# Reading the samples' matrix memories with the queries as a padded stationary operand, and asking for memory rows sooner

## The reference, cut to what matters

```python
qk = jnp.einsum('bthd,bshd->btsh', qc, kc) * W
num = jnp.einsum('btsh,bshd->bthd', qk, vc) + g[..., None] * jnp.einsum('bhvk,bthk->bthv', C, qc)
den = jnp.sum(qk, axis=2) + g * jnp.einsum('bhk,bthk->bth', n, qc)
hc = num / jnp.maximum(jnp.abs(den), jnp.exp(-mt))[..., None]
C = gl[..., None, None] * C + jnp.einsum('bsh,bshv,bshk->bhvk', wl, vc, kc)
```

## Time and profile before

| | |
|---|---|
| median of three runs | 2119.77 us (2115.84 to 2128.39) |
| profiled execution, its own time | 2122.74 us |
| its span, first to last instruction | 2120.9 us |
| PE busy | 1957.2 us, 92% of the span |
| DVE, ACT busy | 1316.9 us (62%), 937.2 us (44%) |
| mean granted clock of TensorE | 0.923 of full speed |

### The profile page before, as it was taken

One profiled execution on the slowest core, in us unless ns is written; L12 is line 12 of the kernel. 1 busy time (PEld: TensorE's weight loads), 2 busy tenths in 40 slices (PEclk: granted clock), 3 DMA queues, 4 the chain that ended last, 5 costly groups with the idle time before them and its releaser, 6 DMA issues.

```text
span 2120.9 us, 28589 instructions
## 1 busy us (share of the span) xinstructions
PE 1957.2 (92%) x10524; PEld 1564.2 (74%) x10524; DVE 1316.9 (62%) x1730; ACT 937.2 (44%) x1259; POOL 120.1 (6%) x162
## 2 busy tenths in 40 slices
PE   5999998799999998999968897999999999999994
PEld 3666665699977477777744585888888888888883
DVE  4352452488742245778833325888888888888884
ACT  0122220000001014676734412777777777777772
POOL 0000000000010000000000001110111100111001
PEclk8999966899999978999979876999999999999997
DMA  4422622445556123333369642999999999999992
GB/s 166 159 80 80 188 65 49 135 161 185 159 167 224 40 79 120 120 125 120 130 224 341 216 144 79 333 358 368 341 338 345 351 361 361 339 336 347 360 374 81
DMA packets 194853, 453.19 MB, mean 214 GB/s; under 512 B 11931, under 2 KB 77591, under 8 KB 193466
## 3 DMA queue, kind: packets, MB, share of 16 engines
q1 hardware_dynamic: 187970, 423.00, 56.6%
q0 software_dynamic: 6784, 28.88, 4.4%
HBM read 439.04 MB, written 21.27 MB: 217 GB/s over the span
## 4 chain that ended last, share of the span: by engine, by line
PE 84%; DVE 8%; DMA 3%; issue 3%; SPq 2%; ACT 1%; POOL 0%; DVEq 0%; POOLq 0%; ACTq 0%
PE bank L2357 76%; PE bank L2360 8%; SPq L2224 1%; DMA arena<-in_cache_nsa 1%; DVE arena L1525 1%; ACT arena L2920 1%; DVE arena L2722 0%; DVE uT L2657 0%; DMA arena<-in_x_sample 0%; DMA arena<-in_cache_nsa_win 0%; DMA ring<-in_cache_nsa 0%; DVE rtmp L2650 0%; DVE arena L2645 0%; DMA ring<-scr_y,mem_all 0%; ACT L2920 0%
## 5 line engine op out<-in xcount | busy, mean ns | idle before, releaser
L2357 PE MATMUL bank<-arena_r 128*128 128x448 f32 (+2 forms) x3296 | 813.1, 361 | 16.8 <-DVE uT_r L652 10.1
L2357 PEld LDWEIGHTS bank<-arena_r 128*128 128x128 f32 x3296 | 607.6, 189 | 92.9 <-issue 15.4
L1810 DVE TENSOR_TENSOR ring_r<-ring,arena_r 128x1792 fp32r<-128x1792 f32 (+1 forms) x216 | 443.6, 2088 | 47.6 <-ACT arena_r L2920 46.3
L2920 ACT ACTIVATE arena_r<-ring 128x1792 fp32r<-128x1792 f32 (+1 forms) x216 | 370.1, 1726 | 164.3 <-PE bank L2357 133.8
L2920 ACT ACTIVATE arena<-bank 64x256 f32<-64x256 f32 (+12 forms) x419 | 179.0, 437 | 446.3 <-PE bank L2357 231.8
L2357 PE MATMUL bank<-arena 128*128 128x256 f32 (+20 forms) x1626 | 275.1, 357 | 6.1 <-ACT arena L2920 3.5
L2357 PE MATMUL bank<-ring_r,arena_r 128*128 128x448 f32 (+1 forms) x840 | 246.1, 374 | 0.0
L2357 PEld LDWEIGHTS bank<-arena 128*128 128x128 f32 (+13 forms) x1626 | 195.8, 182 | 63.0 <-issue 38.0
L2357 PEld LDWEIGHTS bank<-ring_r,arena_r 128*128 128x128 f32 x840 | 157.7, 188 | 21.6
L2360 PE MATMUL bank<-consts_sb,arena 128*128 128x128 f32 (+7 forms) x792 | 134.0, 303 | 40.9 <-DMA arena<-in_x_sample 10.8
L1810 DVE TENSOR_TENSOR arena_r<-arena,arena_r 128x1792 fp32r<-128x1792 f32 (+1 forms) x72 | 138.5, 1936 | 52.3 <-ACT arena_r L2920 51.0
(11 more groups left out here) (358 smaller groups left out, 1762.5 us busy)
## 6 DMA issues: line engine op xcount, KB each, us to landing
ring<-in_w_moe_gu SPq DMA_DIRECT2D x144, 896.0 KB, 6.9
ring<-in_w_moe_d SPq DMA_DIRECT2D x60, 1024.0 KB, 6.5
ring<-in_cache_nsa SPq DMA_DIRECT2D x176, 256.0 KB, 4.6
arena<-in_w_moe_gu SPq DMA_DIRECT2D x48, 896.0 KB, 5.8
ring<-in_w_ffn_gu SPq DMA_DIRECT2D x22, 1024.0 KB, 7.1
arena<-in_cache_nsa SPq DMA_DIRECT2D x80, 256.0 KB, 5.9
ring<-in_w_in_a SPq DMA_DIRECT2D x8, 1536.0 KB, 7.1
arena<-in_w_moe_d SPq DMA_DIRECT2D x12, 1024.0 KB, 6.3
```

The source lines that it names most:

```text
L1810: V.tensor_tensor(unit_low(c), unit_slot(c), unit_high(c), ALU.subtract).then_inc(S("m_sp"), 1)
L2357: return nc.tensor.matmul(out, lhsT, rhs, start=first, stop=last, **kw_)
L2920: return nc.scalar.activation(out, in_, fn, **kw_)
```

## The change

The samples' read is turned around. The query of a half head is now the stationary operand: a block of 32 columns per step n, of which four hold the queries of the four samples and 28 are zero (`qpad`, 16 blocks of 32 columns, cleared once by DVE and filled by one ACT copy). The four turned memories of the step move past it: 384 columns in one matmul. The result is 32 rows x 384 columns, written to one of four strips of 32 partitions of bank 7 or bank 3. Of it only the blocks are wanted in which query b meets memory b. When four steps have filled a bank, ACT copies it to `read` (128 x 384, signal `rd_ev`), and `state_pick(g)` picks the wanted rows: for each b a matmul with `read[:, g % 2, b, :]` (128 x 96) stationary and four columns of the identity moving, into bank 4. `state_pick(2)` stands twice in the order, once in the loop at n = 16 and once behind it.

The stage now starts with two more waits, on the last prompt head's copy (`hp`) and the last output gate's copy (`o_ev`), since banks 3 and 4 are used. Squares go into `og` in place of `sq`. The queries' copy waits for `bT_ev` in place of `cvo_mm`. POOL asks for the keys of samples 4 to 7 and the values of 0 to 3 at once behind the gate biases, for the keys of 0 to 3 when the second norm's sums are done (`nrm_mm` 2), and only then stores the prompt's memory keys and values.

```diff
-        qcol = area(MD, MH, TS)
-        area(MD, TP - MH * TS)
+        area(MD, TP)
+        qpad = arena[0:MD, 16 * MD:16 * MD + 512].rearrange("p (n c) -> p n c", n=16)
+        read = area(P, 2, 4, MD)
 (PE)
                 pe.wait_ge(S("sT_ev"), n + 1)
+                s_ = 32 * (n % 4)
+                mm((bank[7], bank[3])[n // 4 % 2][s_:s_ + 32, 0:384], qpad[:, n, :],
+                   csT[:, n % 2, :, :].rearrange("p b k -> p (b k)")).then_inc(S("sr_mm"), 1)
+
+            def state_pick(g):
+
+                pe.wait_ge(*done("rd_ev", g + 1))
                 for b in range(4):
-                    a = TS * h + 4 * half + b
-                    m = mm(bank[7][0:MD, a:a + 1], csT[:, n % 2, b, :], qcol[:, h, 4 * half + b:4 * half + b + 1])
-                m.then_inc(S("sr_mm"), 1)
+                    a = P + 16 * g + b
+                    mm(bank[4][0:MD, a:a + 13:4], read[:, g % 2, b, :], ident[:, b:P:32])
 
             pe.wait_ge(S("c_ev"), 8)
+            pe.wait_ge(S("hp"), MH)
+            pe.wait_ge(*done("o_ev", MH))
             for n in range(2 * MH + 2):
...
                 if n >= 2:
                     state_read(n - 2)
+                if n >= 8 and n % 4 == 0:
+                    state_pick(n // 4 - 2)
+            state_pick(2)
+            state_pick(3)
 
             pe.wait_ge(*done("bd"))
-            pe.wait_ge(*done("o_ev", 8))
...
-                m = mm(bank[0][0:MH, 0:NT], csel[0:MD, h, :], sq[0:MD, h, :], h == 0, h == MH - 1)
+                m = mm(bank[0][0:MH, 0:NT], csel[0:MD, h, :], og[:, h, :], h == 0, h == MH - 1)
 (DVE)
             out_a()
+            link(V.memset(qpad, 0.0))
             dve.wait_ge(*done("bT_mm"))
...
-            dve.wait_ge(S("sr_mm"), 2 * MH)
-            link(V.tensor_tensor(hT[:, :, TP:NT], bank[7][0:MD, 0:64].rearrange("p (h b) -> p h b", h=MH),
+            link(V.tensor_tensor(hT[:, :, TP:NT], bank[4][0:MD, P:P + 64].rearrange("p (h b) -> p h b", h=MH),
 (ACT)
-            act.wait_ge(*done("cvo_mm", 4))
-            link(f(qcol, qk[:, 0:MH, TP:NT], ACT.Copy), "q_col")
+            act.wait_ge(*done("bT_ev"))
+            link(f(qpad.rearrange("p (h a) c -> p h a c", a=2)[:, :, :, 0:4],
+                   qk[:, 0:MH, TP:NT].rearrange("p h (a c) -> p h a c", a=2), ACT.Copy), "q_col")
...
                 link(f(csT[:, n % 2, :, :].rearrange("p b k -> p (b k)"), bank[5 + n % 2][0:MD, 0:384], ACT.Copy), "sT_ev")
+                if n >= 4 and n % 4 == 0 or n == 2 * MH - 1:
+                    g = (n - 1) // 4
+                    act.wait_ge(S("sr_mm"), 4 * g + 4)
+                    link(f(read[:, g % 2, :, :].rearrange("p b k -> p (b k)"), (bank[7], bank[3])[g % 2][:, 0:384], ACT.Copy), "rd_ev")
 (POOL)
+            mem_load_half(load, "mks", "k", 1, og_place)
+            mem_load_half(load, "mvs", "v", 0, hT_place)
+            pool.wait_ge(S("nrm_mm"), 2)
+            mem_load_half(load, "mks", "k", 0, front)
             mem_store(pool, store, 0)
-            pool.wait_ge(*done("qk_mm", 2))
-            mem_load_half(load, "mks", "k", 0, front)
-            pool.wait_ge(*done("qk_mm", 4))
-            mem_load_half(load, "mks", "k", 1, og_place)
-            pool.wait_ge(*done("qk_mm", 6))
-            mem_load_half(load, "mvs", "v", 0, hT_place)
```

More of the change, by code:

```diff
@@ L65 @@
     "gated": (("ff_si", 22), ("m_si", 48)),
-    "once_act": (("ms_e0", 1), ("q_col", 1), ("o_si", 1), ("hn_rt", 1), ("gates", 3), ("ms_e1", 1), ("pc_e0", 1), ("pc_te", 1), ("pc_e", 2),
+    "once_act": (("ms_e0", 1), ("q_col", 1), ("o_si", 1), ("rd_ev", 4), ("hn_rt", 1), ("gates", 3), ("ms_e1", 1), ("pc_e0", 1), ("pc_te", 1), ("pc_e", 2),
                  ("cm_e", 1), ("rt_e", 1), ("f_ss0", 1), ("f_ss1", 1), ("f_rs0", 1), ("f_rs1", 1), ("f_ss2", 1), ("f_rs2", 1)),
@@ L2840, in sample_sum @@
                 if h == 5:
-                    link(V.tensor_tensor(sq[0:MD, :, 0:TP], hT[:, :, 0:TP], hT[:, :, 0:TP], ALU.mult))
+                    link(V.tensor_tensor(og[:, :, 0:TP], hT[:, :, 0:TP], hT[:, :, 0:TP], ALU.mult))
             dve.wait_ge(S("nd_mm"), MH)
@@ L2854, in _ @@
             link(V.tensor_copy(gb[:, 1, :, :].rearrange("p b c -> p (b c)"), bank[4][0:MD, 0:64]))
-            dve.wait_ge(S("sr_mm"), 2 * MH)
-            link(V.tensor_tensor(hT[:, :, TP:NT], bank[7][0:MD, 0:64].rearrange("p (h b) -> p h b", h=MH),
+            link(V.tensor_tensor(hT[:, :, TP:NT], bank[4][0:MD, P:P + 64].rearrange("p (h b) -> p h b", h=MH),
                                  gb[:, 1, :, :].rearrange("p b h -> p h b"), ALU.mult))
             link(V.tensor_tensor(hT[:, :, TP:NT], hT[:, :, TP:NT], og[:, :, TP:NT], ALU.mult))
-            link(V.tensor_tensor(sq[0:MD, :, TP:NT], hT[:, :, TP:NT], hT[:, :, TP:NT], ALU.mult), "hsq")
+            link(V.tensor_tensor(og[:, :, TP:NT], hT[:, :, TP:NT], hT[:, :, TP:NT], ALU.mult), "hsq")
             dve.wait_ge(*done("hn_rt"))
```

## The result

The changed kernel takes 2125.08 us (median of 20 runs, 2122.15 to 2128.84) beside 2120.25 for the kernel before (20 runs). The ratio is 1.003, with a 95% interval of 1.0018 to 1.0042: slower by 4 to 9 us, within the 0.5% that the prediction called no change, and some 4 us under its 2129.0. The profiled execution took 2127.57 us, its span is 2125.8, its mean granted clock 0.927 (before 2122.74, 2120.9, 0.923).

A forecast was written before the change was run, and what follows sets the result against it. PE alone was taken to bound the samples' stage, at clock 0.50. Read +2.9, picks +6.3 and memset +0.05 gave +9.2 us on the median 2119.77, so 2129.0 us, 0.43% slower; range 2117 to 2138.

The forecast's parts named there:

- The read: Samples' stage on PE: a step's read goes from 1.26 to 1.44 us, sixteen times, +2.9 us (ends +0.3 and +6.4).
- rival 2: Samples' read: form switches at their dearest, 1.66 us a read, +12.8 us in all, 2132.6 us; chance 0.18.
- The pick: `state_pick` on PE, five times: 40 instructions at 0.158 us, +6.3 us, upper end +8.4.
- What costs nothing: ACT's extra copies, new entry waits and the last pick's wait are covered; the `qpad` memset on DVE adds +0.05 us.
- The memory rows: POOL's earlier memory loads: already in time, so gain 0, and no contention with weight loads, so loss 0.
- The stage: Samples' stage: the spread of 1/den starts 9 us later after the stage's start than 54.75.
- the signs that the prediction names: Samples' stage: clock 0.50, pitch 3.6 to 3.7 us, read 1.4 to 1.5, eight picks 1.26; first 130 us agree to tenths.
- The step that failed: Samples' stage: PE never waits there, so time added to PE's order goes on the end, all +9.2 us.
- Rival 1: Samples' stage: the new reads raise the clock to 1.00, -20.8 us, 2099.0 us; chance 0.14, whole or in part.
- Rival 3: The change does not do what it says; picks overlapped down to nothing would leave +2.9 us, 2122.7; chance 0.05.

The follow-up runs named there:

- wide: Changed kernel with the read's stationary block 96 columns wide instead of 32, the samples' read result left out; 2124.89 us, one run.
- one_pick: Changed kernel without the second `state_pick(2)` behind the loop; 2130.81 us, ratio 1.0046 to the kernel before.
- rows_only: Kernel before with only POOL's order of memory row loads and stores taken from the changed kernel; 2118.29 us, ratio 0.9989.
- read_only: Changed kernel with the memory row loads at their old place; 2127.32 us, ratio 1.0035 to the kernel before.
- a_fill: Changed kernel with PE's two waits at the stage's start filled by 264-column matmuls, sums still of 8 rows; 2131.09 us, ratio 1.0054 to the kernel before.
- a_pad_fill: Changed kernel with sums zero-padded to 128 rows and PE's two entry waits filled by 264-column matmuls; 2104.52 us, ratio 0.9941 to the kernel before.
- a_pad2: Changed kernel with 128-row sums, zeros written behind PE's signal, no filling, group 2 picked once; 2105.93 us, ratio 0.992 to the kernel before.
- b_pad2: Kernel before, one-column reads kept, with 128-row sums, zeros written behind PE's signal, waits not filled; 2113.57 us, ratio 0.997.
- b_pad: Kernel before, one-column reads kept, with sums zero-padded to 128 rows, waits not filled; 2110.67 us, ratio 0.9946.

## Why the prediction was right, and where it was not

The time lay where it was forecast, in the stage, on PE, at 0.50, and the verdict within 0.5% held. That it held is in part luck: two errors of opposite sign made it look better than its terms. The stage grew by more than was forecast, and by the forecast's own rule that all of it goes on the end the time would have been 2131.2 us (2119.77 + 11.4), past the 2130.4 from which it says slower; less came through than went in.

**The read.** Taken as 1.44 us, measured 1.42. My reason for going under the sum's 1.52, that 32 columns load faster than 96, fell with wide. The term was mis-sized for another cause: I put both changes of form into the read, and one of them shows on the turns. A step lost 0.16 + 0.14 = 0.30 us, so 16 x 0.30 = +4.8 where I had +2.9. By its effect the read costs 1.56, past the 1.53 from which rival 2 was to decide; rival 2 did not come in the total only because of what was given back later. For the estimate one has to count the changes per step (two before, three after), whichever instruction carries them. The Trainium skill (TensorEngine Tiling (Array Packing), Key Properties) says that a change of tiling mode drains the engine; the 0.14 us of after and wide fit that, though the traces show the price and not what it is paid for.

**The pick.** Taken as 0.158 us per instruction from loads of 96 x 96, measured 0.171 for eight with 128 x 96 (1.37 us, one_pick) and 0.166 for sixteen (2.65, after); with 96 rows it is 0.158 for eight before an 8-row sum (312.03 to 313.29, wide) and 0.159 for sixteen (344.01 to 346.55, wide). The 128-row picks are dearer by 0.11 us for eight and for sixteen alike, so that is paid once for a run of picks and not with each load; what it is paid for is open. Five groups are +6.8 us, not +6.3.

**What costs nothing.** Right: no wait for ACT before the reads or the last pick, none at the entry beyond before's. The second `state_pick(2)` did cover ACT's copy (0.64 us). The memset of `qpad` took 0.48 us at 214.28, in DVE's wait.

**The memory rows.** Right: 0, by rows_only and read_only.

**The stage.** +4.8 + 6.8 = 11.6 by the terms, +11.4 by the stage's length; forecast +9.2. Not forecast at all: the head norm's sums behind it lose the early rise of the clock, +1.3. By the signs that the prediction names, the pitch was 3.75 us for 3.6 to 3.7, eight pick instructions 1.37 for 1.26, the growth 11.4 for 9; the clock, the read's own two instructions and the first 130 us (129.50 for 129.19) were as forecast.

**The step that failed** is the first one, that time added in a stage where PE never waits goes on the end. In the profiled executions 13.2 us were added by the head norm's end and 4.9 reached the end of the span; by the ratios the changed kernel lost 6.4 us in all, and of the 11.5 us of plain delay 6.4 reached the time. I had read that PE never waits in the stage and took it that nothing behind could give anything back. The clock behind it did: three groups of matmuls ran wholly or for the most part at 1.2 GHz in before and wholly or partly at 2.4 in after. That accounts for 5.5 of the 8.3 us that came back in the traces. What sets the time at which the clock falls or rises there is left open.

**Rival 1** did not come, and a_fill beside a_pad_fill bears out the reason named against it, an eight-row matmul in every step. But the idea was good. a_fill shows that keeping the clock up over the entry isn't enough with 8-row sums; a_pad2 that with 128-row sums the turned reads keep it at 1.00, to 17 us faster than before, where I had worked out 20.8 for the rise. No run has such steps begin at 0.50, so whether they would raise the clock, and not only hold it, is open. Rival 3's free picks fell, since each was paid.

## What to carry to other kernels

Where a stage is bound by PE at half clock and has matmuls over few rows in it, zero rows up to 128 are worth a try: the streaming takes no longer (1.37 us for 1.52 here), and together with streaming neighbours the clock may stay up. With the turned reads this gave 0.8% (0.6% with the filling). Padding alone shortened the stage by 7 us in b_pad2 and 5 in b_pad, and in b_pad, whose zeros are written ahead of PE's signal, nothing of it was left at the spread of the roots; the 0.5% by which b_pad was faster came from behind the stage. Count the changes of tile form per step and price each, also where the neighbour carries it. Before putting a stage's added time on the end one for one, put a known delay at the same place: in this kernel 11.5 us cost 6.4 and 23.1 cost 23, so a difference of some microseconds between two versions can come from where later waits meet the clock.

## What the runs showed of the hardware that was not expected

- A pair of 384-column matmuls over 128 rows takes 1.37 us (301.57 to 302.94, b_pad2), over 8 rows 1.52, both at 0.50.
- The clock stayed at 1.00 over the same entry waits (1.23 and 1.03 us) when the two sums between had 128 rows (b_pad, a_pad2, b_pad2) and fell when they had 8.
- With padded sums the clock fell behind a wait of 1.27 us among 96 x 1 reads (b_pad2) and held over one of 1.02 among 96 x 384 reads (a_pad2).
- Behind the delays, the same matmuls of the FFN norm took 5.5 us, 3.8 and 5.5 as their start moved from 398.56 to 411.66 to 422.32; from 399.45, 0.9 us behind before's, they took 3.8 (b_pad).
